# A decoder layer on one core: reordered VectorE work in the feed-forwards, four slots of rounded weights, a fourth unit in the second half's down blocks

## The reference, cut to what matters

```python
def rmsnorm(x, g):
    y = x * lax.rsqrt(jnp.mean(x * x, axis=-1, keepdims=True) + EPS)
    return y * g

def swiglu(h, w_gate, w_up, w_down):
    return (jax.nn.silu(h @ w_gate) * (h @ w_up)) @ w_down

h = rmsnorm(x, ffn1_norm)
x = x + 0.5 * swiglu(h, ffn1_w_gate, ffn1_w_up, ffn1_w_down)
proj = rmsnorm(x, mix_norm) @ w_in          # then the two groups of the mixer
...
x = x + memory_xattn(rmsnorm(x, xattn_norm), rmsnorm(mem, mem_norm), ...)
h = rmsnorm(x, ffn2_norm)
x = x + 0.5 * swiglu(h, ffn2_w_gate, ffn2_w_up, ffn2_w_down)
```

## Time and profile before

| | |
|---|---|
| median of 3 runs | 1881.78 us (1881.56 to 1881.98) |
| the profiled execution, first to last instruction | 1880.3 us |
| around it, to the median of the runs | 1.5 us |
| TensorE matmuls busy | 1874.0 us (100%), 8808 matmuls |
| VectorE busy | 1606.9 us (85%), 2077 instructions |
| ScalarE busy | 1096.4 us (58%), 1496 instructions |
| GpSimd busy | 95.2 us (5%) |
| granted TensorE clock | 1.000 |
| HBM traffic | 192 GB/s over the span |

### The profile page before, as it was taken

The page is one execution under the profiler, slowest core; times in us unless marked ns, Lnnn a source line. Parts: engine busy times, 40 slices in busy tenths (PEclk is TensorE's granted clock), DMA queues, the critical chain, the costliest instruction groups (busy, mean ns, idle before and its releaser), DMA issues.

```text
span 1880.3 us, 23355 instructions
## 1 busy us (share of the span) xinstructions
PE 1874.0 (100%) x8808; PEld 1570.5 (84%) x8808; DVE 1606.9 (85%) x2077; ACT 1096.4 (58%) x1496; POOL 95.2 (5%) x98
## 2 busy tenths in 40 slices
PE   9999999999999999999999999999999999999999
PEld 8888888888889888988888888888888888888987
DVE  6999999989999868787677764789999999999986
ACT  7665555555656547556476655656555565555553
POOL 0000000000000002312260000000000000000000
PEclk9999999999999999999999999999999999999999
DMA  9666655666556664456443654456555566665654
GB/s 338 224 197 200 195 197 194 226 202 201 180 184 211 219 230 155 137 165 227 144 152 108 220 184 136 157 190 195 197 192 194 199 209 214 201 199 183 194 193 171
DMA packets 176753, 362.58 MB, mean 193 GB/s; under 512 B 8576, under 2 KB 19840, under 8 KB 176000
## 3 DMA queue, kind: packets, MB, share of 16 engines
q1 hardware_dynamic: 176208, 360.89, 57.6%
q10 hardware_dynamic: 432, 0.19, 0.0%
HBM read 358.95 MB, written 2.10 MB: 192 GB/s over the span
## 4 chain that ended last, share of the span: by engine, by line
PE 88%; DVE 9%; issue 2%; ACT 1%; DMA 0%; DVEq 0%; SPq 0%; ACTq 0%
PE acc L2090 16%; PE acc L2092 16%; PE acc L2091 16%; PE acc L2079 8%; PE acc L2081 8%; PE acc L2080 8%; DVE w_lo L1376 5%; PE small L2090 2%; PE small L2092 2%; PE small L2091 2%; PE small L2291 2%; PE tr L2038 2%; PE tr L2090 1%; PE tr L2092 1%; PE tr L2091 1%
## 5 line engine op out<-in xcount | busy, mean ns | idle before, releaser
L1376 DVE TENSOR_TENSOR w_lo<-w_raw,w_hi 128x1024 fp32r<-128x1024 f32 (+3 forms) x784 | 760.2, 1025 | 52.8 <-ACT w_hi L765 40.5
L765 ACT ACTIVATE w_hi<-w_raw 128x1024 fp32r<-128x1024 f32 (+4 forms) x566 | 497.6, 916 | 132.3 <-PE acc L2092 105.9
L2090 PE MATMUL acc<-w_hi,hT_hi 128*128 128x512 f32 (+1 forms) x960 | 371.0, 386 | 0.1
L2092 PE MATMUL acc<-w_lo,hT_hi 128*128 128x512 f32 (+1 forms) x960 | 368.9, 384 | 0.0
L2091 PE MATMUL acc<-w_hi,hT_lo 128*128 128x512 f32 (+1 forms) x960 | 368.6, 384 | 0.0
L870 ACT ACTIVATE w_hi<-w_raw 128x1024 fp32r<-128x1024 f32 (+1 forms) x192 | 198.7, 1045 | 125.7 <-DVE w_raw L1364 76.9
L1305 DVE TENSOR_TENSOR w_lo<-w_raw,w_hi 128x1024 fp32r<-128x1024 f32 (+1 forms) x166 | 197.1, 1229 | 24.9 <-ACT w_hi L765 23.3
L863 ACT ACTIVATE w_hi<-w_raw 128x512 fp32r<-128x512 f32 (+1 forms) x192 | 155.7, 831 | 92.3 <-PE acc L2092 89.0
L2090 PEld LDWEIGHTS acc<-w_hi,hT_hi 128*128 128x128 f32 x960 | 180.2, 188 | 34.9 <-DVE w_lo L1376 0.6
L2092 PEld LDWEIGHTS acc<-w_lo,hT_hi 128*128 128x128 f32 x960 | 180.2, 188 | 34.2
L2091 PEld LDWEIGHTS acc<-w_hi,hT_lo 128*128 128x128 f32 x960 | 180.3, 188 | 33.3
(11 more groups left out here) (344 smaller groups left out, 2628.8 us busy)
## 6 DMA issues: line engine op xcount, KB each, us to landing
w_raw<-in_ffn_w_down SPq DMA_DIRECT2D x56, 768.0 KB, 4.7
w_raw<-in_ffn_w_down SPq DMA_DIRECT2D x40, 1024.0 KB, 5.3
w_raw<-in_ffn_w_gate SPq DMA_DIRECT2D x58, 512.0 KB, 3.9
w_raw<-in_ffn_w_gate SPq DMA_DIRECT2D x38, 768.0 KB, 4.4
w_raw<-in_ffn_w_up SPq DMA_DIRECT2D x38, 768.0 KB, 4.5
w_raw<-in_w_in SPq DMA_DIRECT2D x28, 1024.0 KB, 5.1
w_raw<-in_ffn_w_up SPq DMA_DIRECT2D x54, 512.0 KB, 4.8
w_raw<-in_ffn_w_up SPq DMA_DIRECT2D x26, 1024.0 KB, 5.9
```

The source lines that it names most:

```text
L765: nc.scalar.activation(piece(w_hi, c % SPLIT, k0, k1, width), piece(raw, c % RAW, k0, k1, width), ACT.Copy).then_inc(hi_done, 1)
L1376: v.tensor_tensor(piece(w_lo, c % RAW, k0, k1, width), piece(raw, c % RAW, k0, k1, width), piece(w_hi, c % SPLIT, k0, k1, width).bitcast(F ...
L2090: mm(dst, lhs_hi, wh, start=first, stop=False)
L2092: return mm(dst, lhs_hi, wl, start=False, stop=last)
```

## The change

It does the following.

- SPLIT goes from 3 to 4, with 4 KB more in the slab and a smaller scratch area for descriptors. H_SUMS goes from 3 to 4 and A_SUMS from (5, 3) to (5, 4): a fourth token sum of h, and of the activations in the second half.
- `Duo` has a list `later` of its own for the side-1 slots. The second half's down blocks have four units and plain slots of 3, 3, 3 and 2 tiles. Up blocks stay at three units. The mixer's pair has side-1 slots of 4, 2 and 2 tiles in place of four of 2.
- `combine` and `lo_parts` are cut into `first_sums` (L1364), `other_sums` (L1366, then the w_lo split of the raw slot's first tile, then L1368), `other_raw`, `made_lo` and `plain_lo`. Two-tile slots are rounded and split by one instruction each.
- VectorE's order: `first_sums` of a unit goes ahead of the w_lo of the plain slot before it, with `multiply_up` and `turn_round_lo(m, 1)` behind that slot, then `other_sums`; `turn_round_lo(m, 0)` goes between `other_sums` and `other_raw`. `first_sums` of the next Duo goes ahead of the last plain slot, `take_first` behind it. ScalarE's SiLU goes behind `hi_raw` of the next Duo.
- `take_parts` has three operations; TensorE no longer restarts the P5 accumulator but goes on adding to it, and in the first side-1 slot it does all tiles of token tile 0 before it waits for `parts_taken`.

```diff
-SPLIT = 3
+SPLIT = 4
...
+    H_SUMS, A_SUMS = 4, (5, 4)
...
+        UP3 = ("upupup", [0, 2, 4], [(6, 4), (10, 3), (13, 3)], [(6, 4), (10, 3), (13, 3)])
+        DOWN = [("upupupupup", [0, 2, 4, 6, 8], 2 * [(10, 3), (13, 3), (16, 3), (19, 3), (22, 2)]),
+                ("upupupup", [0, 2, 4, 6], 2 * [(8, 3), (11, 3), (14, 3), (17, 2)])]
...
@@ ScalarE @@
             def hi(c, rep, tiles, width, part=None):
                 c += rep
+                if tiles == 2:
+                    act.wait_ge(loaded[c % RAW], landed(c))
+                    act.wait_ge(slot_used, freed(c, 1))
+                    nc.scalar.activation(piece(w_hi, c % SPLIT, 0, 2, width), piece(raw, c % RAW, 0, 2, width), ACT.Copy).then_inc(hi_done, 2)
+                    return
...
-                    for n, (k, tiles) in enumerate(d.plains):
-                        if d.up and n == 2:
-                            for t in range(TT):
-                                act.wait_ge(ev("first_taken"), TT * m + t + 1)
-                                nc.scalar.activation(gate[:, t, 0:w], gate[:, t, 0:w], ACT.Silu,
-                                                     scale=cols(rsq, NAMES[f], t, 1)).then_inc(ev("gated"), 1)
+                    for n, (k, tiles) in enumerate(d.later):
                         hi(d.seconds[n], 0, tiles, w)
...
                         hi_raw(e.raws[0], e.width)
+                        if d.up:
+                            for t in range(TT):
+                                act.wait_ge(ev("first_taken"), TT * m + t + 1)
+                                nc.scalar.activation(gate[:, t, 0:w], gate[:, t, 0:w], ACT.Silu,
+                                                     scale=cols(rsq, NAMES[f], t, 1)).then_inc(ev("gated"), 1)
...
@@ VectorE @@
+            def first_sums(c, width, made_sem="combined"):
+                b, made = weight_tiles(c, width), weight_tiles(c + 1, width)
                 dve.wait_ge(loaded[c % RAW], landed(c))
                 dve.wait_ge(slot_used, 2 * (c + 1 - RAW + 1))
                 v.tensor_tensor(made[:, 0:2, :], b[:, 1:4:2, :], b[:, 0:2, :], ALU.subtract).then_inc(ev(made_sem), 1)
+            def split(c, i, k0, k1, width):
+                dve.wait_ge(hi_done, 2 * c + i + 1)
+                return v.tensor_tensor(piece(w_lo, c % RAW, k0, k1, width), piece(raw, c % RAW, k0, k1, width),
+                                       piece(w_hi, c % SPLIT, k0, k1, width).bitcast(F32), ALU.subtract)
+            def other_sums(c, n, width, made_sem="combined"):
+                b, made = weight_tiles(c, width), weight_tiles(c + 1, width)
                 dve.wait_ge(ev(made_sem), 2 * n + 1)
                 done(v.tensor_tensor(made[:, 2, :], b[:, 3, :], made[:, 0, :], ALU.subtract))
+                split(c, 0, *RAW_PARTS[0], width).then_inc(lo_done, 1)
                 done.wait()
                 v.tensor_tensor(made[:, 3, :], b[:, 2, :], made[:, 2, :], ALU.subtract).then_inc(ev(made_sem), 1)
+            def other_raw(c, n, width, made_sem="combined"):
+                dve.wait_ge(ev(made_sem), 2 * n + 2)
+                split(c, 1, *RAW_PARTS[1], width).then_inc(lo_done, 1)
+            def made_lo(c, width):
+                for i, (k0, k1) in enumerate(MADE_PARTS):
+                    split(c, i, k0, k1, width).then_inc(lo_done, 1)
...
             def take_parts(m):
...
-                done(v.tensor_tensor(gate[:, 1, 0:w], p7, nat[:, 0, 0:w], ALU.add))
-                done(v.tensor_tensor(nat[:, 0, 0:w], p5, nat[:, 0, 0:w], ALU.add))
-                done.wait()
-                v.tensor_tensor(nat[:, 1, 0:w], p5, gate[:, 1, 0:w], ALU.add).then_inc(ev("parts_taken"), 1)
+                done(v.tensor_tensor(nat[:, 1, 0:w], p7, nat[:, 0, 0:w], ALU.add))
+                v.tensor_tensor(nat[:, 0, 0:w], p5, nat[:, 0, 0:w], ALU.add).then_inc(ev("parts_taken"), 1)
...
                         if kind == "u" and n:
-                            combine(d.raws[n], u0 + n, w)
-                            lo_parts(d.raws[n], RAW_PARTS, w, u0 + n)
+                            first_sums(d.raws[n], w)
+                            if d.order[:2 * n].endswith("p"):
+                                plain_lo(d.firsts[n - 1], d.plains[n - 1][1], w)
+                                if n == 1 and m > m0 and DUOS[m - 1].up:
+                                    multiply_up(m - 1)
+                                if n == 2 and turns_in(d):
+                                    turn_round_lo(m, 1)
+                            other_sums(d.raws[n], u0 + n, w)
                             if n == 1 and turns_in(d):
                                 turn_round_lo(m, 0)
-                            lo_parts(d.raws[n] + 1, MADE_PARTS, w)
+                            other_raw(d.raws[n], u0 + n, w)
+                            made_lo(d.raws[n] + 1, w)
...
-                    for n, (k, tiles) in enumerate(d.plains):
-                        if n == 2:
+                    for n, (k, tiles) in enumerate(d.later):
+                        if n == len(d.later) - 1:
+                            if m < LAST[f]:
+                                first_sums(DUOS[m + 1].raws[0], DUOS[m + 1].width)
                             if not d.up:
                                 add_parts(m)
-                            take_first(m)
-                        lo_parts(d.seconds[n], PLAIN_PARTS[tiles], w)
+                        plain_lo(d.seconds[n], tiles, w)
...
+                    take_first(m)
                     if m < LAST[f]:
                         e = DUOS[m + 1]
-                        combine(e.raws[0], u0 + u1, e.width)
+                        other_sums(e.raws[0], u0 + u1, e.width)
...
@@ TensorE @@
+                if side == 1 and n == 0:
+                    for kk in range(tiles):
+                        half(kk)
+                        tile(kk, 0)
+                    pe.wait_ge(ev("parts_taken"), m + 1)
+                    for kk in range(tiles):
+                        ins = tile(kk, 1)
+                        if kk in (mid - 1, tiles - 1):
+                            ins.then_inc(slot_used, 1)
+                    return
```

More of the change, by code:

```diff
@@ L94 @@
     plains: list
+    later: list
     raws: list = field(default_factory=list)
@@ L115, in place @@
                 c += 1
-        for n in range(len(self.plains)):
+        for n in range(len(self.later)):
             self.seconds.append(c)
@@ L433, in layer @@
         PARTS = [small[:, 0, :], small[:, 1, :], tr[:, 1, :]]
[L434 to L437 removed]
+        short = [c for d in DUOS + [PAIR] for slots_, plains in ((d.firsts, d.plains), (d.seconds, d.later))
+                 for c, (_, tiles) in zip(slots_, plains) if tiles == 2]
         def freed(c, i):
@@ L2161, in plain, with tile, half @@
                 d = DUOS[m]
-                c, (k0, tiles), w = (d.firsts, d.seconds)[side][n], d.plains[n], d.width
+                c, (k0, tiles), w = (d.firsts, d.seconds)[side][n], (d.plains, d.later)[side][n], d.width
                 hi_, lo_ = (hT_hi, hT_lo) if d.up else (actT_hi, actT_lo)
-                last, mid = n == len(d.plains) - 1, (tiles + 1) // 2
-                for kk in range(tiles):
+                last, mid = n == len((d.plains, d.later)[side]) - 1, (tiles + 1) // 2
+                def tile(kk, t):
+                    at_ = slice(t * P, (t + 1) * P)
+                    return product(acc[:, GB[d.f] if side == 0 else 1 - GB[d.f], t, 0:w], hi_[:, k0 + kk, at_], lo_[:, k0 + kk, at_], c, kk, w,
+                                   False, last and kk == tiles - 1, goes_on=side == 1 and t == 1)
+                def half(kk):
                     if kk in (0, mid):
```

166 lines of the change are left out of this document (83 added, 83 removed).

## The result

The changed kernel takes 1896.46 us, median of 4 runs (1895.96 to 1897.02), the kernel before 1881.86 beside it. The ratio is 1.0078 with a 95% interval of 1.0063 to 1.0092: slower by 14.6 us, well beyond the 0.2% that can be told apart. The profiled execution took 1895.96 us and has a span of 1894.1, at a granted clock of 1.00. The forecast was 1894.1, between 1885 and 1901.

What follows compares the result with a forecast made beforehand. The prediction took TensorE's instruction stream as the bound. Its terms -2.7 - 3.1 + 16.1 + 2.0 gave +12.3 us on a median of 1881.8, so 1894.1 us, range 1885 to 1901 (chance 0.74).

Steps and rivals of the forecast that it cites:

- round trip: Unit 1 of turning blocks: other_raw waits behind VectorE, ScalarE, VectorE; chain 11.37 us against TensorE's 11.21; +16.1 us over both feed-forwards.
- 12 matmuls fewer: Second half's down blocks, both feed-forwards: a fourth unit saves 12 matmuls at 0.225 us, -2.7 us on TensorE's path.
- removed waits: TensorE's waits for parts and some w_lo splits go: 14 or so at 0.22 us, -3.1 us, between 0 and -5.1.
- wide up block, no flat copy: Second product of unit 1 comes 0.16 us late, plus 0.11 for resuming: 0.27 us each, three per feed-forward.
- wide up block with flat copy: ScalarE makes the flat copy first, 0.49 us more: 0.76 us each, four per feed-forward.
- narrow up block: Block of 384 columns: chain 9.68 us against TensorE's distance of 8.64; cost 1.15 us.
- first half's down block 0: First plain slot has 3 tiles, so TensorE comes at 9.86 us against a chain of 10.84; cost 1.1 us.
- second half's down block 0: Chain 10.30 us on time costs 0.56; VectorE put late by 1.37; 1.9 us, between 0.56 and 3.3.
- The opening: First block of FFN1: chain with the fourth hS_lo ends at 63.54 against 61.67; +2.0 us, between 0.3 and 2.5.
- the edge: Down blocks with the fourth unit: VectorE 49.1 us against TensorE's 48.9; if it falls behind, 0.2 us a block shows.
- Rival 2: At other_raw of unit 1 the chain is under 11.2 us, so the kernel ends faster, 1876.0 us; chance 0.12.
- Rival 4: VectorE becomes the bound; staying 1.37 us late at block starts lengthens every chain, +27 us, 1921; chance 0.06.

Runs made afterwards that it cites:

- e1: The changed kernel with only turn_round_lo(m, 0) moved back behind other_raw; 1881.78 us, 0.9998 of the kernel before.
- e2: The kernel before with only turn_round_lo(m, 0) put between the two w_lo splits of unit 1's raw tiles; 1904.53 us, 1.0119.
- e3: The changed kernel with ScalarE's turn_round_hi(m, 0) between the halves of hi_made of unit 1, VectorE untouched; 1884.33 us, 1.0011.
- e11: The changed kernel with ScalarE rounding two tiles of the next plain slot (0.95 us) ahead of turn_round_hi(m, 0); 1917.97 us, 1.0189.
- e4: e1 with three units again in the second half's down blocks, 12 matmuls more; 1881.90 us, 0.9999.
- e5: e1 with first block's plain split ahead of first_sums, FFN1's last add_parts behind the last split, three units in second half's down block 0; 1880.38 us, 0.9996.
- e6: e5 but four units in both second-half down blocks, and turn_round_hi(m, 0) between the halves of hi_made; 1880.50 us, 0.9994.
- e10: e9 without its ScalarE change: turn_round_hi(m, 0) stays behind both halves of hi_made; 1878.92 us, 0.9982.
- e9: e1 with first_sums later in first blocks, add_parts and take_first one slot earlier, three units in down block 0, turn_round_hi(m, 0) between hi_made's halves; 1878.30 us, 0.9979.
- e12: e1 with four units in the up blocks too, 60 matmuls fewer; 1913.87 us, 1.0169.

## Why the prediction was right

The mechanism and the size were right: the time is the round trip ahead of other_raw. What the runs set against it fell (e1, e2, e3, e11). Step by step, forecast and measured, in us, the second from the start distances:

| step | forecast | measured |
|---|---|---|
| 12 matmuls fewer | -2.7 | -2.7 |
| removed waits, both feed-forwards (before less e4, opening and last block left out) | -3.1 | -3.0 |
| wide up block, no flat copy (6) | 0.27 | 0.25 |
| wide up block with flat copy (8) | 0.76 | 0.73 to 0.76 |
| narrow up block (2) | 1.15 | 1.13 |
| first half's down block 0 (2) | 1.1 | 1.08 |
| second half's down block 0 | 1.9 each | 2.4 and 1.5 |
| first block of FFN1 | +2.0 | +2.2 |
| last down block of FFN1 | not seen | +0.7 |
| mixer, attention and first 20 us | not seen | +0.3 |

These add up to 13.2 or 13.3 of the 13.7 us; the rest lies in starts that are each late by less than 0.1. The removed waits came out at the forecast by luck: in the trace of before seven are clear, of 0.28 to 0.39 us each (2.4 together), and the rest is in smaller ones, where I had taken fourteen of 0.22.

The chain from TensorE's end to the product was put at 11.37 us; it is 1428.83 - (1417.52 - 0.04) = 11.35. TensorE's own pace reaches it after 11.21 by the forecast, and 11.19 now.

Three steps were off. **The opening** has the right sum, but I put all of it on the round trip (63.54 against 61.67). The round trip is there and ends at 63.87, where the product starts at once. But by then TensorE has only 0.2 us left to wait: it has already lost 0.6 at slot 7 behind the fourth hS_lo, and 1.24 where first_sums (L1378) now stands ahead of the first plain split. VectorE cannot be early in that block, so a reorder that I had priced at nothing costs its whole duration. The costs lie one over the other, so that e1, without the round trip, gets back at most 0.5 us here; e5, with first_sums back behind the split as well, gets back some 1.2 more. The 0.6 is not the fourth hS_lo alone: at the same place, with the same instructions, e1 waits 0.2 us, e6 0.7 and e5 and e10 not at all. VectorE and TensorE of after:

```profile
54.59 1.23 DVE L1378 TENSOR_TENSOR w_raw<-w_raw 128x1024 f32<-128x1024 f32 x1 [0.32 <-DVE stage L1493]
55.73 2.35 DVE L1383 TENSOR_TENSOR w_lo<-w_raw,w_hi 128x1024 fp32r<-128x1024 f32 x2
...
62.60 2.35 DVE L1383 TENSOR_TENSOR w_lo<-w_raw,w_hi 128x1024 fp32r<-128x1024 f32 x2
```
```profile
57.01 0.50 PE L2129 MATMUL acc<-w_hi,hT_hi 128*128 128x512 f32 x1 [0.97 <-DVE w_lo L1383]
...
63.87 0.50 PE L2129 MATMUL acc<-w_hi,hT_hi 128*128 128x512 f32 x1
```

The earlier trace rows shows the old order: the split began at 53.64. **The last down block of FFN1** was missed: the forecast has no term for add_parts and take_first, and in this block VectorE also makes hT_lo. e9, with both of them one slot earlier, has no wait there. **The four units** were priced as a saving with "the edge" named beside it and left out of the sum. e4 shows 3.1 us of waits for 2.7 us saved. Part of them my 1.9 per block held, as 0.56 of the chain and a lateness of 1.37 carried over from other blocks. VectorE and TensorE's last product of the block before, at the block's start:

```profile
599.41 1.01 DVE L1430 TENSOR_TENSOR stage<-acc,stage 128x384 f32<-128x384 f32 x2
...
1791.38 1.01 DVE L1430 TENSOR_TENSOR stage<-acc,stage 128x384 f32<-128x384 f32 x2
```
```profile
597.15 0.33 PE L2131 MATMUL acc<-w_lo,hT_hi 128*128 128x384 f32 x1
...
1790.25 0.33 PE L2131 MATMUL acc<-w_lo,hT_hi 128*128 128x384 f32 x1
```

VectorE is late by 1.93 and 0.80 us. With 0.56 that gives 2.5 and 1.4 us, against 2.4 and 1.5 measured: the term was built right, and the size I gave it was the mean of the two by luck.

The rule that TensorE pulls weight loads ahead of matmuls in flight ("TensorE: Matmul & The Clock Gate" of the Trainium skill, the specification table) does not help here: after each wait the resumed matmul takes 0.50 and the next start follows at 0.34, as in the earlier trace rows. That 0.11 is in every row of the table that counts waits at a product of unit 1.

Rival 2 decided at 11.2 us for the chain; it is 11.35. e3, with the chain some 1.0 us shorter, shows that rival in all up blocks behind the opening. Rival 4 does not hold for this change (VectorE waits for 39.9 us at L1419) and holds in e12. Not tried: the waits left in e9's opening, the fourth hS_lo taken out alone, and first_sums moved back alone in the first block.

## What to carry to other kernels

A statement moved within one engine's queue moves everything behind it to the far side of its wait. Before moving it, follow its wait to the engine that releases it, and on to what that engine waits for: if the trail comes back to the queue you started from, it is a round trip, and its whole length stands in front of the next result. Price it from the other engine's own end, block kind by block kind, since 0.15 us of missing slack is paid at every pass. And a saving on the bound engine counts only less the waits that its preparation brings to the engine that feeds it; look for these at the block's edges, where that engine is already late.

## What the runs showed that was not expected

- A gain and its cost can cancel: e1 and the kernel before differ by 0.1 us in the median (less than the runs of e1 can tell), with 12 matmuls fewer, the old waits gone, and others of the same sum in their place.
- A wait removed at one instruction came back whole at the next, on another releaser (0.59 us on w_lo in e1, 0.60 on what must be take_first in e5), because both stood in one stretch of VectorE that was late.
- The 11 runs of e1 spread from 1880.58 to 1883.52, the 4 of after lay within 1.1 us. The traces show waits in the first 20 us that come and go, 2.8 us in e1 and 4.1 in e10, between kernels whose instructions there are the same; in e10 and e5 ScalarE sits idle there for loads.
